# Filler steps of an in-projection, grouped behind each level's update

## The reference, cut to what matters

```python
proj = u @ w_in
qkv_a, z_a, b_a, a_a, qkv_b = jnp.split(proj, [3 * DA, 4 * DA, 4 * DA + HA, 4 * DA + 2 * HA], axis=-1)
...
kb = kc * bc[..., None]
lower = jnp.where(strict, jnp.einsum("nbhid,nbhjd->nbhij", kb, kc) * decay, 0.0)
sol = lax.linalg.triangular_solve(lower + eye, rhs, left_side=True, lower=True, unit_diagonal=True)
u_c, w_c = sol[..., :dv], sol[..., dv:]
qk = jnp.where(incl, jnp.einsum("nbhid,nbhjd->nbhij", qc, kc) * decay, 0.0)
def step(S, xs):
    v_new = u_n - jnp.einsum("bhck,bhkv->bhcv", w_n, S)
    o = jnp.einsum("bhck,bhkv->bhcv", qd_n, S) + jnp.einsum("bhij,bhjv->bhiv", qk_n, v_new)
    S = S * gl_n[..., None, None] + jnp.einsum("bhck,bhcv->bhkv", kd_n, v_new)
```

## Time and profile before

| what | us |
|---|---|
| three runs, median | 2914.39 |
| the profiled execution | 2910.33 |
| its span | 2908.5 |
| TensorE busy in the span | 2766.9 (95%) |
| ScalarE busy in the span | 617.7 (21%) |
| VectorE busy in the span | 1242.4 (43%) |
| GpSimd busy in the span | 997.8 (34%) |

### The profile page before, as it was taken

The page is one execution under the profiler, slowest core; times in us unless marked ns, Lnnn a source line. Parts: engine busy times, 40 slices in busy tenths (PEclk is TensorE's granted clock), DMA queues, the critical chain, the costliest instruction groups (busy, mean ns, idle before and its releaser), DMA issues.

```text
span 2908.5 us, 45166 instructions
## 1 busy us (share of the span) xinstructions
PE 2766.9 (95%) x18337; PEld 2633.5 (91%) x18337; DVE 1242.4 (43%) x2134; ACT 617.7 (21%) x1087; POOL 997.8 (34%) x406
## 2 busy tenths in 40 slices
PE   7999899989999999999999978699999999999996
PEld 7999788867889999999999878599999999999996
DVE  4655565556053444444432524920442222222234
ACT  4221333356241000010000331320520000000002
POOL 4444111000343433333333314434424443333330
PEclk7999899989999999999999989799999999999998
DMA  4236312110231222222222246842221111111102
GB/s 139 88 103 128 92 59 75 37 67 23 83 103 60 75 86 84 81 81 81 81 82 83 77 113 156 280 119 59 95 94 44 44 50 50 43 43 43 44 30 78
DMA packets 156979, 236.61 MB, mean 81 GB/s; under 512 B 57664, under 2 KB 120384, under 8 KB 153664
## 3 DMA queue, kind: packets, MB, share of 16 engines
q1 hardware_dynamic: 52400, 137.18, 15.3%
q10 hardware_dynamic: 104464, 97.77, 11.1%
HBM read 174.96 MB, written 64.16 MB: 82 GB/s over the span
## 4 chain that ended last, share of the span: by engine, by line
PE 36%; issue 35%; POOL 15%; DMA 5%; DVE 4%; ACT 2%; ACTq 1%; POOLq 0%; SPq 0%; DVEq 0%
POOL w_hi L699 10%; PE psum L729 8%; PE psum L730 7%; PE psum L731 7%; POOL w_lo L702 6%; DMA stage<-wstream 4%; PE psum L789 2%; PE psum L1178 2%; PE psum L1150 1%; PE psum L1004 1%; PE psum L1165 1%; PE psum L1025 1%; DVE area L2041 1%; DMA area<-s 1%; DVE area L2056 1%
## 5 line engine op out<-in xcount | busy, mean ns | idle before, releaser
L729 PE MATMUL psum<-x_hi,w_hi 128*128 128x344 f32 (+3 forms) x3600 | 1176.2, 327 | 33.4 <-DVE x_lo L2065 23.9
L730 PE MATMUL psum<-x_lo,w_hi 128*128 128x344 f32 (+3 forms) x3600 | 1159.1, 322 | 0.0
L731 PE MATMUL psum<-x_hi,w_lo 128*128 128x344 f32 (+3 forms) x3600 | 1157.5, 322 | 0.0
L699 POOL TENSOR_TENSOR w_hi<-stage,const 128x1024 fp32r<-128x1024 f32 x193 | 487.7, 2527 | 1734.4 <-PE psum L731 1710.3
L729 PEld LDWEIGHTS psum<-x_hi,w_hi 128*128 128x128 f32 x3600 | 686.1, 191 | 45.6 <-DVE x_lo L2065 21.6
L730 PEld LDWEIGHTS psum<-x_lo,w_hi 128*128 128x128 f32 x3600 | 686.2, 191 | 3.5 <-issue 1.7
L731 PEld LDWEIGHTS psum<-x_hi,w_lo 128*128 128x128 f32 x3600 | 685.4, 190 | 0.0
L702 POOL TENSOR_TENSOR w_lo<-stage,w_hi 128x1024 fp32r<-128x1024 f32 x193 | 485.5, 2516 | 15.1
L729 PE MATMUL psum<-act_hi,w_hi 128*128 128x344 f32 (+2 forms) x1056 | 343.9, 326 | 19.8 <-DVE area L2536 15.2
L2523 DVE TENSOR_TENSOR area<-area,psum 128x344 f32<-128x344 f32 (+2 forms) x132 | 67.7, 513 | 654.5 <-ACT area L1811 654.3
L731 PE MATMUL psum<-act_hi,w_lo 128*128 128x344 f32 (+2 forms) x1056 | 338.9, 321 | 0.0
(11 more groups left out here) (224 smaller groups left out, 2108.4 us busy)
## 6 DMA issues: line engine op xcount, KB each, us to landing
stage<-wstream SPq DMA_DIRECT2D x193, 512.0 KB, 3.6
s_set<-area ACTq DMA_DIRECT2D x8, 1860.0 KB, 7.9
area<-s SPq DMA_DIRECT2D x8, 1348.0 KB, 7.3
proj<-area ACTq DMA_DIRECT2D x20, 520.0 KB, 2.7
area<-proj ACTq DMA_DIRECT2D x36, 256.0 KB, 4.1
resid<-area ACTq DMA_DIRECT2D x6, 1376.0 KB, 6.1
area<-resid ACTq DMA_DIRECT2D x6, 1376.0 KB, 8.5
area<-s SPq DMA_DIRECT2D x8, 1024.0 KB, 7.5
```

Source lines behind the costliest of these rows:

```text
L699: pool.tensor_tensor(per_block(w_hi[:, slot, :]), src, ones_block, ALU.mult).then_inc(high_split, 1)
L729: mm(out[:, 0:n], w_hi[:, slot, wk], hi[:, xk, a:a + n], start=first, stop=False)
L730: mm(out[:, 0:n], w_hi[:, slot, wk], lo[:, xk, a:a + n], start=False, stop=False)
L731: return mm(out[:, 0:n], w_lo[:, slot, wk], hi[:, xk, a:a + n], start=False, stop=last)
```

## The change

A gap is now one for each level, behind the update and the pieces behind it, with four steps. The gap between product and update is gone. ScalarE's list is not reordered; its formula for the gap takes the new numbers.

```diff
-FILL_STEPS = 2
+FILL_STEPS = 4
...
             def dn_level(n, lev, between_products=(), behind=()):
-                gap = 2 * (LEVELS - 1) * (n - 1) + 2 * (lev - 1)
+                gap = (LEVELS - 1) * (n - 1) + lev - 1
                 dn_level_p(n, lev)
-                fill(gap)
                 for f, *args in between_products:
                     f(*args)
                 dn_level_up(n, lev)
                 for f, *args in behind:
                     f(*args)
-                fill(gap + 1)
+                fill(gap)
...
             def filled_evac_at(n, lev):
 
-                gap = 2 * (LEVELS - 1) * (n - 1) + 2 * (lev - 1)
+                gap = (LEVELS - 1) * (n - 1) + lev - 1
                 steps = 3 * KT + FILL_STEPS * gap
                 if gap > 0 and steps % KT == 0 and steps <= (N_PROJ - FIRST_FILLED) * 3 * KT:
                     filled_evac(steps // KT - 1)
```

## The result

The changed kernel takes 2984.55 us (median of 4, 2981.55 to 2989.83) against 2916.29 for the kernel before beside it: ratio 1.023, interval 1.0211 to 1.0249, so 68 us slower. Forecast were 2972 with a range of 2946 to 2992. The profiled execution took 2982.49, its span is 2980.7, 72.2 above the span before.

The account below looks back on a forecast made before the run. TensorE, busy throughout a steady DeltaNet block, was taken as the bound. Waits of 47.1 us plus clock dips of 10.2 us, 57.3 together, on the median 2914.4 gave 2972 us, range 2946 to 2992.

Parts of the forecast that it names:

- the main line: DeltaNet blocks: waits of 47.1 us plus about one clock dip a block, 2972 us; chance 0.50.
- rival (b): Two clock dips a block, or dips of 14 us as behind block 8: 2982 to 2997; chance 0.14.
- the waits: TensorE waits over all DeltaNet blocks, 7.25 us in each of blocks 2 to 6: together 47.1 us.
- TensorE's queue is the price of the stage: DeltaNet: TensorE busy all 32.98 us of a steady block, so any wait put into its queue is added whole.
- The product copies stay covered: Blocks 2 to 7: pieces of 0.53 to about 1.0 us hide ScalarE's 0.38 us copy of each product.
- Switching saves 0.1 a block: TensorE: one filler run fewer per level saves on switches; 0.1 us a block taken, bounds 0 and 1.2.
- The held group copy: ScalarE's filler evacuation delays its queue: 3.65 us from level 1, 1.05 level 3, 1.87 level 5, 0.78 ahead of qk.
- The clock, 10.2 us: One dip of TensorE's granted clock in each of blocks 2 to 7, 1.7 us each: 10.2 us.
- Outside DeltaNet nothing changes: Expected sign in the profile after: everything outside the DeltaNet stage unchanged.
- The rule on brief idling: Skill page: TensorE idling briefly and often swings between two clocks and pays each swing; read as at least one dip a block.
- The stretch 570 to 585: Earlier trace, block 8: clock held 1.00 through gaps of about 0.5 us; by it alone 2962 us.

Follow-up runs that it names:

- the waits filled: Changed kernel with matmuls nobody reads put into TensorE's waits of blocks 1 to 7; 2958.78 us, ratio 1.0162.
- the early Exp: As late copy, plus the Exp for q moved ahead of level 6's product copy on ScalarE; 2914.90 us, ratio 1.0002.
- late copy: Changed kernel with ScalarE's filler group copy moved behind the product copy of the next level; 2923.95 us, ratio 1.0032.
- The hold alone: Kernel before, two steps a gap kept, filler started one gap later so groups end behind the update; 2952.63 us, ratio 1.0133.

## Why the prediction was right, and where a size was off

- *The time, 2972.* 2984.55 lies in the range, but not where the main line put it. Two dips a block is rival (b), with 2982 to 2997, to which I gave 0.14; about one dip a block had 0.50. The range held because its upper end was drawn to the middle of (b). What was foreseen is the waits: 47.1 us, against 44 measured (2958.78 with the waits filled, less 2914.59).
- *TensorE's queue is the price of the stage; each wait is added whole.* Held: the 7.16 us of waits in a block (1.03, 2.48, 1.01, 1.94, 0.70) lengthen it by 7.28 once the clock is out of it (40.26 less 32.98).
- *The product copies stay covered.* Held: the early Exp shows no wait at all with nothing but the pieces between, late copy none but the one ahead of qk.
- *Switching saves 0.1 a block.* 0.2 to 0.3 (32.98 to between 32.70 and 32.79); of no weight.
- *The held group copy.* Held in place, releaser and size. At level 2, 1.03 and 2.48 of idle time, 5.34 from product to update where 5.35 was worked out. At level 4 1.01 for 1.05, at level 6 1.94 for 1.87, ahead of qk 0.70 for 0.78. Taking the distances of ScalarE's chain from the earlier trace rows, one of them estimated for level 3, and hanging them on the new moment at which the group ends was all it needed. Block 1, with the time at half clock taken out, is some 3 us longer; 3.2 was worked out.
- *The clock, 10.2 us.* This is the term that was mis-sized. Instead of one dip a block there are two places, one behind update 6 and one at update 2, and one of them lasts 6.8 us: 10.2 us at half clock in a block, of which some fall into the waits and cost nothing. It measures 4.0 a block instead of 1.7, and 26 us over all (2984.55 less 2958.78; 24 when each is set against the kernel before beside it) instead of 10.2. The missing 12 us of the forecast are here. I had put the two dips into rival (b) at 0.14 on the ground that dense fillers follow level 6; they do follow, but at half clock, since the dip came behind the wait and not at it.
- *Outside DeltaNet nothing changes.* Held within 2.4 us.
- *The rule on brief idling* in the Trainium skill ("TensorE: Matmul & The Clock Gate", section "A second HAM failure mode: psum-queue depth-cycling"): the trace of the changed kernel agrees, with dips in every steady block at waits of 0.7 to 2.5 us, gone with the waits filled (1.00 in 412.58:452.84). The page gives no number of dips; one a block was my reading of it, and two came. The hold alone shows that it isn't so in each block: with waits of 2.34, 0.93 and 0.70 the clock held 1.00 through two of them. The stretch 570 to 585 of the earlier trace rows, which I had set against the rule, had gaps of 0.5 only.

## What to carry to other kernels

When work of one engine is moved in its list, look in the other engines' lists for the waits that name its end: an engine that works through its list in order holds everything written behind such a wait, and what it holds is what the first engine needs next. The consumer's place in the list must move with the producer's; here one changed call was worth 59 of 68 us. And where an engine with a falling clock must wait anyway, price the clock beside the wait: here some 2 us for each pair of waits of 2.6 to 3.5 us, and nothing in some blocks with the hold alone.

## What the runs showed of the hardware that I had not expected

TensorE's time went down as it was given more to do: 26 calls more in a block, 52 matmuls in the trace, made it 4.0 us shorter, at granted clock 1.00 against 0.88. Nearly the same waits gave dips of 3.4 us in one block and 6.8 in the next, and none in two blocks with the hold alone. Three load issues of ScalarE took 1.99 us behind the copy of v and 1.49 behind a product copy. A copy of four columns on VectorE took 1.25 us instead of 0.17 where a GpSimd instruction ran beside it.
